# Sigmoids by tanh, both keys of a round normed in one visit, rotated features copied by ScalarE: a decoder step on one core

## The reference

```
xn = rms_norm(x); split(xn @ w_in) -> aq ak av az mq mk mv mo mz ga gm mi mf
aq, ak = partial_rope(rms_norm(.., per head), pos)      # the first 32 of 128 features are rotated
prompt: causal attention over the own block of 256; sampled tokens: attention over
        the top 3 of 4 cached blocks (1024 cached keys, by block mean) and the new token
mLSTM in chunks of 64 (prompt), one state update (sampled tokens)
h = rms_norm(h * sigmoid(mo)); y_att = (attn * silu(az)) @ w_proj_attn
y_ml = (h * silu(mz)) @ w_proj_mlstm
y = x + (sigmoid(ga) * y_att + sigmoid(gm) * y_ml) @ w_out
```

## Time and profile before

| | us |
|---|---|
| median of 3 runs | 477.28 (477.18 to 478.46) |
| the profiled execution, whole | 477.14 |
| its span, first to last instruction | 475.0 |
| TensorE busy | 462.9 (97%) |
| VectorE busy | 403.4 (85%) |
| ScalarE busy | 290.2 (61%) |
| GpSimd busy | 101.8 (21%) |
| DMA | 150.86 MB, mean 318 GB/s |

### The profile page before, as it was taken

How to read it: one execution, slowest core, us unless ns; L and a number is a source line. 1 busy time by engine, 2 the same in 40 slices (tenths; PEclk the granted TensorE clock), 3 DMA queues, 4 the chain that set the end, 5 groups by cost and what they waited for, 6 DMA issues and landing times.

```text
span 475.0 us, 11339 instructions
## 1 busy us (share of the span) xinstructions
PE 462.9 (97%) x3860; PEld 422.3 (89%) x3860; DVE 403.4 (85%) x1650; ACT 290.2 (61%) x486; POOL 101.8 (21%) x181
## 2 busy tenths in 40 slices
PE   6999999999989999999999999999999999999997
PEld 4899899998779898888899889899898898899997
DVE  4898899699999898999899999789999954567861
ACT  4866545666964584994485695657848368334430
POOL 2031321013223223422321332312223110000000
PEclk9999999999999999999999999999999999999999
DMA  8697589657999999999999999998999996446511
GB/s 310 257 392 290 211 307 339 219 200 246 313 418 409 412 366 322 337 398 414 413 386 352 386 398 393 417 383 309 344 420 410 415 412 213 172 172 236 186 79 47
DMA packets 36665, 150.86 MB, mean 318 GB/s; under 512 B 5232, under 2 KB 6772, under 8 KB 29312
## 3 DMA queue, kind: packets, MB, share of 16 engines
q1 hardware_dynamic: 12304, 70.77, 39.2%
q0 software_dynamic: 19008, 67.20, 37.1%
q10 hardware_dynamic: 5296, 12.18, 6.6%
HBM read 137.37 MB, written 12.76 MB: 316 GB/s over the span
## 4 chain that ended last, share of the span: by engine, by line
PE 72%; DVE 12%; ACT 9%; issue 3%; DMA 3%; ACTq 0%; SPq 0%; DVEq 0%
PE pj L533 26%; PE pj L536 13%; PE wk L533 8%; PE pa L726 5%; PE wk L536 4%; DVE w L1056 3%; DVE kpages L1155 3%; ACT w L812 2%; DMA out_C_s<-cslot 2%; DVE cslot L1243 2%; ACT L832 2%; PE wk L486 2%; PE wk L638 2%; PE wk L670 1%; DMA cst<-in_consts 1%
## 5 line engine op out<-in xcount | busy, mean ns | idle before, releaser
L533 PE MATMUL pj<-xn,w 128*128 128x264 f32 x1328 | 180.9, 289 | 0.4 <-ACT mqT L965 0.4
L533 PEld LDWEIGHTS pj<-xn,w 128*128 128x128 f32 x1328 | 168.5, 189 | 8.5 <-issue 6.8
L1056 DVE TENSOR_TENSOR w<-wraw,w 128x1024 fp32r<-128x1024 f32 x112 | 136.9, 1226 | 11.0 <-ACT w L812 10.5
L812 ACT ACTIVATE w<-wraw 128x1024 fp32r<-128x1024 f32 x112 | 117.8, 1053 | 25.2 <-PE wk L536 12.8
L1155 DVE CUSTOM_DVE_ANT_0 kpages<-kpages,qbc 128x128 f32<-128x128 f32 x512 | 114.7, 288 | 1.6 <-DMA kpages<-in_cache_k 1.4
L536 PE MATMUL pj<-xn,w 128*128 128x264 f32 x664 | 94.2, 284 | 3.7 <-DVE w L1056 3.7
L536 PEld LDWEIGHTS pj<-xn,w 128*128 128x128 f32 x664 | 85.5, 188 | 4.6 <-DVE w L1056 4.6
L403 POOL DMA_DIRECT2D kpages<-in_cache_k x64 | 34.3, 536 | 178.4 <-DVE sco L1155 154.6
L403 POOL DMA_DIRECT2D vpages<-in_cache_v x64 | 33.9, 529 | 67.2 <-issue 37.3
L1155 DVE DVE_READ_ACCUMULATOR2_ANT sco<- 128x1 f32 x512 | 41.7, 81 | 0.0
L726 PE MATMUL pa<-vpages,prob 128*32 128x256 f32 x512 | 34.3, 385 | 0.8 <-ACT prob L870 0.8
(11 more groups left out here) (279 smaller groups left out, 658.3 us busy)
## 6 DMA issues: line engine op xcount, KB each, us to landing
wraw<-in_weights SPq DMA_DIRECT2D x56, 1024.0 KB, 7.9
kpages<-in_cache_k POOLq DMA_DIRECT2D x64, 512.0 KB, 8.0
vpages<-in_cache_v POOLq DMA_DIRECT2D x64, 512.0 KB, 10.3
cslot<-in_states SPq DMA_DIRECT2D x16, 512.0 KB, 10.5
out_C_s<-cslot ACTq DMA_DIRECT2D x16, 512.0 KB, 8.0
xres<-in_tokens SPq DMA_DIRECT2D x1, 1056.0 KB, 7.2
out_k_p<-kT ACTq DMA_DIRECT2D x4, 256.0 KB, 11.6
out_v_p<-v_nat ACTq DMA_DIRECT2D x4, 256.0 KB, 6.5
```

Of the source, the lines that this page charges most:

```text
L533: mm(bank[:, 0:T], w2[:, q, 0, k, :], src[:, g, k, :], start=(k == 0 and g == 0), stop=False)
L812: A(w2[:, n % WSPLIT, 0], wraw[:, pair % WRAW, :, (n % 2) * P:(n % 2 + 1) * P], ACT.Copy).then_inc(whi_ready, 1)
L1056: V.tensor_tensor(w2[:, q, 1], wraw[:, slot, :, half * P:(half + 1) * P], w2[:, q, 0], ALU.subtract).then_inc(wlo_ready, 1)
```

## The change

- Every Sigmoid becomes a Tanh of half the argument: sigmoid(x) = (1 + tanh(x/2)) / 2. The halves are put into the evacuations' scale (0.5 for mo, az, mz), into the mLSTM norm's weight and the last product's scalar; the products with a gate become `scalar_tensor_tensor` with (t + 1).
- The features of each attention head come in another order (`ORDER`), so that the two halves of the rotated features start at partitions 0 and 32. The order is in the weights, the norm weights, the constants and the outputs, on the host.
- The product with `rot` is gone. ScalarE copies the two groups of 32 partitions crosswise (`swap`) into one of four places in `zsig`; the sign is in `sin`. VectorE's first three operations of `rope_norm` work on 64 partitions only, the first from SBUF.
- Sampled queries go back to the usual order by a product with the matrix `back` instead of a transpose.
- Both keys' sums are formed at TensorE's step 2 (which comes after projection 3); ScalarE does both norms at step 4, the two Lns, then the two Exps. VectorE's rotations are at steps 4 and 5, the scores at 5 and 6, the softmax maxima at 6 and 7.
- The gate rows are all computed at h = 0 of the queries' stage.

```diff
+        swapped = [zsig[0:2 * LO, a, c, :] for a in range(2) for c in range(2)]
...
-            def norm_sums(ss, ro, i, src):
-                mm(ss[:, 0:T], ones, sq[:, i, :], start=True, stop=True)
-                mm(ro[:, 0:T], rot, src, start=True, stop=True).then_inc(norm_ps, 1)
+            def norm_sums(ss, i):
+                mm(ss[:, 0:T], ones, sq[:, i, :], start=True, stop=True).then_inc(norm_ps, 1)
...
                     if g >= 2:
-                        pe.wait_ge(q_ready, g - 1)
-                    norm_sums(wk[2 * (g % 2)], wk[2 * (g % 2) + 1], g % 2, qT[:, g, :])
+                        pe.wait_ge(rs_ready, g - 1)
+                    norm_sums(wk[2 * (g % 2)], g % 2)
...
-                    last = tr(bank[0:NB, (h - first) * P:(h - first + 1) * P], qT[:, h, SEQ:T], P)
+                    last = mm(bank[0:NB, (h - first) * P:(h - first + 1) * P], qT[:, h, SEQ:T], back, start=True, stop=True)
...
-                if i in (1, 3):
-                    n = i // 2
-                    pe.wait_ge(evac, HEADS + j * CHUNKS + n + 1)
...
-                    norm_sums(wk[2 * n], wk[2 * n + 1], n, kT[:, n, :])
-                if i in (4, 6):
-                    n = i // 2 - 2
+                if i == 2:
+                    pe.wait_ge(evac, HEADS + j * CHUNKS + 2)
+                    pe.wait_ge(c_ready, NB * j) if j else pe.wait_ge(qs_ready, 2)
+                    for n in range(2):
+                        norm_sums(wk[2 * n], n)
+                if i in (5, 6):
+                    n = i - 5
                     pe.wait_ge(kT_ready, 2 * j + n + 1)
...
+            def swap(x, place):
+                ch.join()
+                A(place[0:LO], x[LO:2 * LO], ACT.Copy)
+                A(place[LO:2 * LO], x[0:LO], ACT.Copy).then_inc(swap_ready, 1)
...
+                if 1 <= h < HEADS:
+                    act.wait_ge(swap_read, max(0, h - 3))
+                    swap(qT[:, h, :], swapped[h % 4])
...
-                A(zsig[:, 1], zraw[:, 1], ACT.Sigmoid).then_inc(sig_ready, 1)
+                A(zsig[:, 1], zraw[:, 1], ACT.Tanh).then_inc(sig_ready, 1)
...
-                if i in (2, 4):
-                    n2 = i // 2 - 1
+                if i == 4:
                     act.wait_ge(kT_ready, 2 * j)
-                    act.wait_ge(norm_ps, HEADS + 2 * j + n2 + 1)
-                    inv_rms(wk[2 * n2][:, 0:T], rs[:, n2, :], HD).then_inc(rs_ready, 1)
+                    act.wait_ge(norm_ps, HEADS + 2 * j + 2)
+                    for n2 in range(2):
+                        ch.step(A(rs[:, n2, :], wk[2 * n2][:, 0:T], ACT.Ln, scale=1.0 / HD, bias=epsc))
+                    ch.join()
+                    for n2 in range(2):
+                        A(rs[:, n2, :], rs[:, n2, :], ACT.Exp, scale=-0.5).then_inc(rs_ready, 1)
...
                 split_hi(n + AHEAD)
+                if i in (0, 2):
+                    act.wait_ge(silu_ready, j)
+                    act.wait_ge(swap_read, HEADS + 2 * j - 2)
+                    swap(kT[:, i // 2, :], swapped[i // 2])
...
-                    A((sga, sgm)[m][:, c, :], banks[i % 4][:, 0:T], ACT.Sigmoid).then_inc(sg_ready, 1)
+                    A((sga, sgm)[m][:, c, :], banks[i % 4][:, 0:T], ACT.Tanh, scale=0.5).then_inc(sg_ready, 1)
...
-                ch.step(V.tensor_tensor(hT[:, 0, :], ro[:, 0:T], sin, ALU.mult))
-                ch.link(V.tensor_tensor(x, x, cos, ALU.mult))
-                ch.link(V.tensor_tensor(x, x, hT[:, 0, :], ALU.add))
+            def rope_norm(x, r, place, done, turn):
+                part = slice(0, 2 * LO)
+                dve.wait_ge(swap_ready, turn + 1)
+                V.tensor_tensor(hT[part, 0, :], place, sin[part], ALU.mult).then_inc(swap_read, 1)
+                ch.link(V.tensor_tensor(x[part], x[part], cos[part], ALU.mult))
+                dve.wait_ge(swap_read, turn + 1)
+                ch.link(V.tensor_tensor(x[part], x[part], hT[part, 0, :], ALU.add))
...
-                if h == 1:
+                if h == 0:
                     dve.wait_ge(gate_ln, 1)
...
-                if i in (2, 4):
-                    n = i // 2 - 1
-                    dve.wait_ge(norm_ps, HEADS + 2 * j + n + 1)
+                if i in (4, 5):
+                    n = i - 4
...
-                if i in (5, 7):
-                    n = i // 2 - 2
+                if i in (6, 7):
+                    n = i - 6
...
-                    V.tensor_tensor(sgm[:, c, :], banks[i % 4][:, 0:T], sgm[:, c, :], ALU.mult).then_inc(ywk, 1)
+                    V.scalar_tensor_tensor(out=sgm[:, c, :], in0=sgm[:, c, :], scalar=1.0, in1=banks[i % 4][:, 0:T],
+                                           op0=ALU.add, op1=ALU.mult).then_inc(ywk, 1)
```

More of the change, by code:

```diff
@@ L237, in build @@
         ones = cst[:, C_ONE:C_ONE + P]
-        rot = cst[:, C_ROT:C_ROT + P]
+        back = cst[:, C_BACK:C_BACK + P]
         mask3 = cst[:, C_MASK:C_MASK + 384]
@@ L939, in _ @@
                     act.wait_ge(evac, n)
-                    A(zraw[:, 2], zraw[:, 2], ACT.Sigmoid).then_inc(sig_ready, 1)
+                    A(zraw[:, 2], zraw[:, 2], ACT.Tanh).then_inc(sig_ready, 1)
                     fade_states(j, 1)
@@ L947, in _ @@
                     act.wait_ge(hmo_ready, j + 1)
-                    A(sq[:, :, :], hT[:, :, :], ACT.Square).then_inc(sqh_ready, 1)
+                    A(sq[:, :, :], hT[:, :, :], ACT.Square, scale=0.5).then_inc(sqh_ready, 1)
                     act.wait_ge(evac, n)
-                    A(zsig[:, 0], zraw[:, 0], ACT.Sigmoid).then_inc(sig_ready, 1)
+                    act.wait_ge(swap_read, HEADS + 2 * j + 2)
+                    A(zsig[:, 0], zraw[:, 0], ACT.Tanh).then_inc(sig_ready, 1)
                 b = due(g, EXP)
@@ L1227, in keys_side @@
                     dve.wait_ge(sig_ready, 3 * j + 2)
-                    V.tensor_tensor(zraw[:, 0], zraw[:, 0], zsig[:, 0], ALU.mult).then_inc(silu_ready, 1)
+                    V.scalar_tensor_tensor(out=zraw[:, 0], in0=zsig[:, 0], scalar=1.0, in1=zraw[:, 0], op0=ALU.add, op1=ALU.mult)\
+                        .then_inc(silu_ready, 1)
                     dve.wait_ge(silu_ready, j + 1)
@@ L1305, in states_side @@
                     ch.join()
-                    V.tensor_tensor(hT[:, :, :], hT[:, :, :], zraw[:, 2], ALU.mult).then_inc(hmo_ready, 1)
+                    V.scalar_tensor_tensor(out=hT[:, :, :], in0=zraw[:, 2], scalar=1.0, in1=hT[:, :, :], op0=ALU.add, op1=ALU.mult)\
+                        .then_inc(hmo_ready, 1)
                 if i == 15:
@@ L1316, in round_close @@
                 dve.wait_ge(sig_ready, 3 * j + 3)
-                ch.step(V.tensor_tensor(zraw[:, 1], zraw[:, 1], zsig[:, 1], ALU.mult))
+                ch.step(V.scalar_tensor_tensor(out=zraw[:, 1], in0=zsig[:, 1], scalar=1.0, in1=zraw[:, 1], op0=ALU.add, op1=ALU.mult))
                 dve.wait_ge(mrs_ready, j + 2)
@@ L1419, in _ @@
                         dve.wait_ge(xres_load, 16)
-                    V.tensor_tensor(yout[:, c, :], banks[(i - 1) % 4][:, 0:T], xres[:, c, :], ALU.add).then_inc(ep_y, 1)
+                    V.scalar_tensor_tensor(out=yout[:, c, :], in0=banks[(i - 1) % 4][:, 0:T], scalar=0.5, in1=xres[:, c, :],
+                                           op0=ALU.mult, op1=ALU.add).then_inc(ep_y, 1)
 def two_sided(x):
@@ L1435, in constants @@
     half = ROT // 2
-    for m in range(half):
-        c[m + half, C_ROT + m] = -1.0
-        c[m, C_ROT + m + half] = 1.0
+    c[np.arange(P), C_BACK + ORDER] = 1.0
     r = np.arange(P)
@@ L1467, in weight_pairs @@
 def weight_pairs(w_in, w_proj_mlstm, w_proj_attn, w_out):
-    cuts = [w_in[:, AQ + 256 * n:AQ + 256 * (n + 1)] for n in range(4)]
-    cuts += [w_in[:, g + 256 * j:g + 256 * (j + 1)] for j in range(JOBS) for g in GROUPS]
+    pair = np.concatenate([ORDER, HD + ORDER])
+    cuts = [w_in[:, AQ + 256 * n + pair] for n in range(4)]
+    cuts += [w_in[:, g + 256 * j + (pair if g == AK else np.arange(256))] for j in range(JOBS) for g in GROUPS]
     for w in (w_in[:, GA:GA + D], w_in[:, GM:GM + D], w_proj_mlstm, w_proj_attn, w_out):
@@ L1513 @@
     y = g["y"].reshape(P, KC, T).transpose(2, 1, 0).reshape(T, D)
-    k_p = g["k_p"].transpose(3, 0, 2, 1).reshape(rows)
+    there = np.argsort(ORDER)
+    k_p = g["k_p"][:, there].transpose(3, 0, 2, 1).reshape(rows)
     v_p = g["v_p"].reshape(JOBS, P, 2, 256).transpose(2, 1, 0, 3).reshape(rows)
```

38 lines of the change are left out of this document (16 added, 22 removed).

## The result

| | before | after |
|---|---|---|
| median, us | 477.58 (476.58 to 478.71, 6 runs) | 483.79 (483.35 to 485.35, 6 runs) |
| profiled execution, us | 477.14 | 483.51 |
| its span, us | 475.0 | 481.4 |

The account below looks back on a forecast made before the run. TensorE and VectorE, both nearly full, were taken to set the time by stretches. Terms -1.96 - 0.90 + 2.0 + 1.84 + 1.57 - 0.5 = +2.05 us on 477.14 gave 479.2 us, range 474.2 to 481.8.

Parts of the forecast that it names:

- The term of +2.0: Round 1: the late first softmax holds ScalarE's evacuation 6, so projection 8 starts 2.0 us later; bounds 0 and +2.6.
- Round 3's +1.57: Round 3: TensorE waits 1.57 us for the late key; +0.76 if a VectorE product beside a GpSimd broadcast were not held.
- The epilogue's -0.5: Epilogue: TensorE's 0.50 us wait for an Exp behind a table load goes.
- if ScalarE and VectorE keep up. They do, with little to spare: Query stage: condition for winning 2.7 us from six rotations, with ScalarE's work at 3.3 us against a 3.36 us head period.
- The gate arithmetic, which the lower bound was made of: Query stage: gate work in one piece, some 3.8 us, might make VectorE late; gain then -1.3 instead of -1.96.
- or if VectorE waits for ScalarE's copies: Closing sign that the prediction is wrong: VectorE waiting for ScalarE's copies for the rotation; no size given.
- the wait (+1.84): Round 2, first scores: the key is ready at 216.06, TensorE wanted it at 214.29, so 1.84 us are added.
- about 3.5 us: Round 2, first scores: forecast size of TensorE's largest gap.
- (A): Rival: TensorE stays fed in the rounds, the key never late, all sixteen rotations count; -6.9, 470.3 us; chance 0.25.
- (B): Rival: one of the three waits in rounds 1 to 3 does not come; 477.2 to 477.6 us, no change; chance 0.30.
- (C): Rival: more waits, three rotation products held and gate work keeping VectorE late in the query stage; +3.4, 482.6 us; chance 0.12.
- (D): Rival: Tanh fetches a set of its own, a load returns ahead of the epilogue's Exp; 479.7 us; chance 0.33 with the forecast.

Follow-up runs that it names:

- c1_vector_cross: e1 with the query heads' ScalarE copies replaced by two crosswise VectorE products a head; 483.06 us, ratio 1.0119.
- e6_straight: Changed kernel with both copies of a head kept but not crossing partitions (rotated features wrong); 484.71 us, one run.
- e2_fill: Changed kernel with unread TensorE products filling two waits, in the query stage and ahead of round 2's first scores; 481.52 us, ratio 1.0088.
- e3: Changed kernel with one straight copy of 64 partitions in place of a head's two crosswise copies (rotated features wrong); 483.9 us, ratio 1.0132.
- e1: Changed kernel with a round's two keys handled in two visits at their old steps again; 478.03 us, ratio 1.0008.
- e5: Kernel before with only the sigmoids made tanh; 477.0 us, ratio 0.9990.
- c2: Keys in two visits as in e1, query heads 0 and 2 crossed by VectorE, the other six by ScalarE's copies; 476.72 us, ratio 0.9983.
- c5: c2 with the Exp of the cache pages' scores moved ahead of the first key's root at step 2; 475.51 us, ratio 0.9957.
- e4: Kernel before with only the one visit for both keys of a round; 485.37 us, ratio 1.0171.
- e7: Changed kernel with the gate arithmetic spread over heads 1, 2 and 3 again; 483.82 us, one run.
- e8: e3 with unread TensorE products filling the waits of rounds 1 and 2; 481.14 us, ratio 1.0083.

## Why the prediction was right or wrong

**Right: what the one visit costs, and by which waits.** The largest gap is at the first scores of round 2, released by a key. Round 1 goes by the late softmax: ScalarE's Exp began at 150.00 (149.87 was worked out) behind 11.15 us of idle time, where the earlier trace rows had 5.80. The term of +2.0 measured 1.76, with one detail off: what TensorE waited for first was not evacuation 6 but `accr` in the same queue. Round 3's +1.57 measured +1.61, with the reason that it gave: a cache page's product stands beside the broadcast now and is held as the rotation's was the earlier trace rows, so the lower bound of +0.76 did not come.

```profile
287.05 1.31 POOL L422 PARTITION_BROADCAST qbc<-qbc  x1
...
287.11 1.25 DVE L1171 CUSTOM_DVE_ANT_0 kpages<-kpages,qbc 128x128 f32<-128x128 f32 x1
```

The epilogue's -0.5 measured -0.59, and all 20 loads went that were to go (36 before, 16 after). The loads are 14 at the norms' lines and one at the first Tanh:

```profile
L832 ACT ACT_TABLE_LOAD x4 | 5.1, 1283 | 0.1
L833 ACT ACT_TABLE_LOAD x4 | 5.1, 1283 | 0.1
L900 ACT ACT_TABLE_LOAD x3 | 3.8, 1283 | 0.1
L903 ACT ACT_TABLE_LOAD x3 | 3.8, 1283 | 0.1
...
L948 ACT ACT_TABLE_LOAD x1 | 1.3, 1283 | 0.0
```

**Wrong: the query stage, by 2.6 us.** The failed step is the condition "if ScalarE and VectorE keep up. They do, with little to spare", which rested on a ScalarE cycle of 3.3 us against TensorE's 3.36.

```profile
20.79 0.46 ACT L827 ACTIVATE qT<-pj,cols 128x264 f32<-128x264 f32 x1
```

```profile
22.16 0.46 ACT L822 ACTIVATE qT<-pj,cols 128x264 f32<-128x264 f32 x1
...
42.80 0.46 ACT L822 ACTIVATE qT<-pj,cols 128x264 f32<-128x264 f32 x1
```

These are head 1's evacuation before, and those of heads 1 and 7 after. First the size of the cycle: the pair of copies was priced at 0.6 us from one copy's row and costs 1.0 (1.33 from Exp to split with it, 0.33 without it in `c1_vector_cross`). The work beside it was priced at 2.72 and is 2.44: idle time counts only what no earlier instruction still covers, and without waits the evacuation overlaps the split by 0.1 and the Ln starts 0.27 behind the Square, not 0.45. Together the cycle is (42.80 - 22.16) / 6 = 3.44, above 3.36. Second, I compared periods and not positions: the first head's copies stand ahead of head 1, whose evacuation starts 1.0 us later than before (22.16 against 20.79, less the 0.33 of the start-up). An engine without slack carries such a delay to the end, and what it is late by for the last head is TensorE's wait. Head 7's evacuation comes 1.9 us later than with one copy (40.58, start-up taken off); six cycles of 3.44 against 3.36 make 0.5 of that, the late start the rest. `e6_straight` shows the second part by itself: its cycle is 3.31, under 3.36, and TensorE waited 1.39 us. With one copy (2.72) it is worked off, and the stage gives 2.93 us up to g = 4, where 2.86 had been forecast. Of the 2.6 us 0.5 are the 1.2 GHz stretch behind the wait. The gate arithmetic, which the lower bound was made of, was innocent. The prediction ended with "or if VectorE waits for ScalarE's copies"; it was ScalarE itself that was late with the evacuations, and VectorE waited 0.48 us a head for the Exp behind them.

**Wrong: round 2, by 1.36 us.** The failed step is that the sum counted the wait (+1.84) and nothing behind it, although the prediction named the gap, "about 3.5 us". The round lost 3.20. The 1.2 GHz behind the wait cost 1.56, by the rows of `e2_fill`; that leaves 1.64 for the wait, near the forecast. No row of before had such a stretch, so its size could not be read there.

**Small:** 0.33 us at the start-up, where kernels with the same code differ by up to 0.6, and 0.36 in round 0: the late softmax also stands ahead of an evacuation there (it ends at 76.10, and projection 8 starts at 76.15), which I had worked out for round 1 alone.

**The rivals.** (A) is out: the key was late in each of the rounds 1 to 3. (B) is out: all three waits came. (C) had the right size (482.6) by the wrong mechanisms. (D) did not happen: Tanh fetched one set in the whole kernel. That a gain in one place was handed back in another (e3) and that the same program part costs 6 or 8 us depending on what stands around it were in none of them.

## What to carry to other kernels

Where two engines are nearly full, moving an operation one step later costs its lateness at every place where the partner wants it: read the new ready time off the row of what stood there, as was done here. When you compare an engine's new period with that of the engine that sets the time, compare their starts too: with little slack left, the delay it starts with stays. And look for TensorE's longest waits, those of 2 us and more here: price the stretch behind each at both clock levels, or fill the wait.

## What the runs showed of the hardware

- **TensorE's clock.** Of the thirteen profiles, those of before, e1, e2, e5, c2 and c5 have no 2 us window under 0.97 between 10 us and 470 us. In the others each stretch at 0.50 stands behind a wait of 1.9 to 5.2 us: after 2.5 and 3.2 (the changed kernel), 2.2 and 3.2 (e3), 2.2 and 2.2 (e4), 2.2, 3.2 and 1.9 (e6), 3.6 (e7), 2.8 (e8), 5.2 (c1). But waits of the same length had none behind them: 2.5 in e1 and e7, 2.2 in the changed kernel, e2 and e7, 2.1 in e4, 2.4 in e3. And e1 had a stretch in five of its ten executions only. What decides among these stays open. Such a stretch cost 0.5 us in the query stage (the changed kernel against e2) and 1.4 to 1.6 in the rounds (round 1, e3 against e8; round 2, the changed kernel against e2). Where products filled the wait, the clock stayed at 1.00 (two places in e2, two in e8).
- The Trainium skill (ScalarE: Activation LUTs, What ACT_TABLE_LOAD costs) speaks of a drain with each switch. The 14 loads at the norms' lines have 0.4 us of idle time ahead of them in all, so no drain shows here either.
- **ScalarE.** Copies of 264 columns take 0.42 us on 32 partitions and 0.41 on 64: two narrow ones cost more than twice one wide one (0.86 to 1.00 us of the cycle against 0.31). An instruction whose input or output starts at another partition than that of the one ahead starts only when that one has ended (0.42 to 0.45 us behind it, against 0.31 to 0.33); this is read off the rows of the changed kernel, e3 and e6.
- **VectorE.** The same at c1's two crosswise products: 0.46 us apart, where the neighbours L1094 and L1095 before start 0.34 to 0.35 apart. And a cached page's product took 1.25 us instead of 0.29 beside a GpSimd broadcast.
